# One hybrid layer with a mixture of experts: router on x, two-best choice by maximum and index instructions, token numbers scattered by GpSimd

## What is computed

```python
x = x + m                                             # m: the mixer's output projection
h = rmsnorm(x, norm_ffn_g)
gp = softmax(h @ w_router_group)                      # 4 groups
gidx, gval = argmax(gp), max(gp)
el = (h @ w_router_expert).reshape(-1, 4, 8)[gidx]    # the 8 experts of that group
tv, ti = top_k(softmax(el), 2); tv = tv / sum(tv)
for e in range(32):                                   # weighted by gval * tv where e was chosen
    out += combine[:, e] * ((silu(h @ w_gate[e]) * (h @ w_up[e])) @ w_down[e])
y = rmsnorm(x + out, norm_final_g)
```

## Time and profile before

| what | us |
|---|---|
| median of 3 runs (811.31 to 813.5) | 812.87 |
| the profiled execution, its own time | 813.58 |
| its span | 811.8 |
| TensorE products busy in the span | 776.9 |
| VectorE / ScalarE / GpSimd busy | 236.1 / 176.7 / 103.0 |
| DMA, mean over the span | 330 GB/s |

### The profile page before, as it was taken

The page is one execution under the profiler, slowest core; times in us unless marked ns, Lnnn a source line. Parts: engine busy times, 40 slices in busy tenths (PEclk is TensorE's granted clock), DMA queues, the critical chain, the costliest instruction groups (busy, mean ns, idle before and its releaser), DMA issues.

```text
span 811.8 us, 10142 instructions
## 1 busy us (share of the span) xinstructions
PE 776.9 (96%) x4170; PEld 447.5 (55%) x4170; DVE 236.1 (29%) x533; ACT 176.7 (22%) x321; POOL 103.0 (13%) x132
## 2 busy tenths in 40 slices
PE   8999999999999999999999999999998998999995
PEld 7888887888888888853333333333332332343332
DVE  4199869492551222531100111011101101101111
ACT  3104333657445000321111101100110010011001
POOL 5200064524200000001101000001000000000004
PEclk9999999999999999999999999999999999999998
DMA  9845587677849963599999999999999999999992
GB/s 328 239 141 192 162 244 217 174 212 195 260 139 385 401 249 146 195 346 429 422 427 397 424 428 424 428 427 424 429 423 430 428 425 426 422 428 422 419 417 82
DMA packets 75270, 268.03 MB, mean 330 GB/s; under 512 B 5710, under 2 KB 37562, under 8 KB 58447
## 3 DMA queue, kind: packets, MB, share of 16 engines
q1 hardware_dynamic: 73378, 264.26, 84.0%
q0 software_dynamic: 528, 1.90, 0.6%
q10 hardware_dynamic: 1317, 1.19, 0.5%
HBM read 259.26 MB, written 8.55 MB: 330 GB/s over the span
## 4 chain that ended last, share of the span: by engine, by line
PE 72%; DMA 14%; SPq 7%; DVE 2%; issue 2%; POOL 1%; ACT 1%; DVEq 0%; POOLq 0%
PE bank L1602 23%; PE bank L1979 19%; PE bank L2017 8%; SPq L537 7%; PE bank L1875 7%; DMA slot<-in_w_expert_gate_dram 5%; DMA slots<-in_w_expert_gate_dram 5%; PE bank L2026 4%; DMA early<-in_norm_final_g_dram 3%; PE bank L1822 2%; DMA slots<-in_w_in_dram 1%; PE bank L1712 1%; PE bank L1943 1%; PE bank L1634 1%; PE bank L2006 1%
## 5 line engine op out<-in xcount | busy, mean ns | idle before, releaser
L1602 PE MATMUL bank<-hT,slots 128*128 128x264 f32 x832 | 189.6, 388 | 0.0
L1979 PE MATMUL bank<-slots,hT 128*64 128x512 f32 x624 | 180.0, 601 | 5.8 <-DMA slots<-in_w_expert_gate_dram 4.1
L1602 PEld LDWEIGHTS bank<-hT,slots 128*128 128x128 f32 x832 | 156.8, 190 | 26.6 <-issue 0.6
L1460 DVE TENSOR_TENSOR early<-early,bank 128x512 f32<-128x512 f32 x16 | 11.0, 687 | 383.4 <-PE bank L1979 383.4
L1979 PEld LDWEIGHTS bank<-slots,hT 128*64 128x64 f32 x624 | 55.2, 138 | 101.4 <-issue 90.7
L2017 PE MATMUL bank<-slots,wrep 128*64 128x512 f32 x304 | 85.7, 595 | 4.2 <-ACT wrep L1028 4.0
L1979 PE MATMUL bank<-slot,hT 128*64 128x512 f32 x208 | 82.8, 594 | 1.6 <-DMA slot<-in_w_expert_gate_dram 1.6
L761 POOL COPY hT<-early 128x512 f32 x30 | 17.5, 612 | 375.4 <-PE bank L1979 290.2
L2026 PE MATMUL bank<-hT,diag 128*128 128x512 f32 x128 | 59.2, 605 | 0.2 <-ACT hT L1040 0.2
L2017 PEld LDWEIGHTS bank<-slots,wrep 128*64 128x64 f32 x304 | 26.9, 137 | 42.4 <-issue 35.3
L1200 DVE SCALAR_TENSOR_TENSOR slot<-slot,rows_buf 128x256 f32<-128x256 f32 x120 | 49.4, 487 | 0.0
(11 more groups left out here) (315 smaller groups left out, 827.0 us busy)
## 6 DMA issues: line engine op xcount, KB each, us to landing
slots<-in_w_expert_down_dram SPq DMA_DIRECT2D x17, 2048.0 KB, 32.3
slots<-in_w_expert_gate_dram SPq DMA_DIRECT2D x15, 2048.0 KB, 27.0
slots<-in_w_expert_up_dram SPq DMA_DIRECT2D x15, 2048.0 KB, 32.0
slots<-in_w_in_dram SPq DMA_DIRECT2D x13, 2048.0 KB, 9.9
slots<-in_w_expert_gate_dram SPq DMA_DIRECT2D x10, 1024.0 KB, 27.3
slot<-in_w_expert_gate_dram SPq DMA_DIRECT2D x5, 2048.0 KB, 31.5
slot<-in_w_expert_up_dram SPq DMA_DIRECT2D x5, 2048.0 KB, 27.5
slot<-in_w_expert_down_dram SPq DMA_DIRECT2D x5, 2048.0 KB, 37.3
```

The source lines that it names most:

```text
L1460: dve.tensor_tensor(act.rearrange("s (f c) -> s f c", f=FT), act.rearrange("s (f c) -> s f c", f=FT), bank[UP][:, :].rearrange("s (c f) -> ...
L1602: last = mm(out, w[:, a, t * P:(t + 1) * P], (hT if c else xgain)[:, a, :], start=(a == 0), stop=(a == KT - 1))
L1979: last = mm(out[sl, :], xe[:, a, sl], expert_view(p, kind, e, a // 4)[:, a % 4, :], start=(a == 0), stop=(a == KT - 1))
```

## The change

- The router's weights are multiplied by the norm's weight once, by GpSimd, and `route` multiplies `xT` by them. `hT` and `h_rows` are not made. The turned rows are rows of x times one over the root; the norm's weight, loaded once more in the order of the experts' rows (`gain8`), is applied where `xe` is made: by VectorE for pair 0, by GpSimd for the others, whose copies become products.
- The sum of squares is made by GpSimd.
- The two experts are found with `max` and `max_index`, three of each, instead of two `first_max`.
- `sel1` and `row_numbers` are gone. GpSimd scatters the token numbers to their places in a DRAM list `listed` with six indirect transfers (one for each token tile and pick), after the list was filled with zeros early in the kernel, and reads the list back into `list_at`, four numbers on each partition. A pick without a place goes to a spare place of its own.
- TensorE's order is: two turned groups, one seat, two turned groups, ranks, the last two turned groups, three seats. ScalarE makes the exponentials before the last two groups, and an exponential on one row ahead of "ms".
- SyncE issues load 18 before the token rows are stored and load 17 before load 19.

```diff
+LISTED = 5 * P
...
+        gain8 = vec[:, 68:76]
...
-        tok_id = sb("tok_id", [P, 3])
+        tok_id = sb("tok_id", [P, 3], I32)
+        list_pos = sb("list_pos", [P, 3, 2], U32)
...
+        top = flat(24).rearrange("p (a n) -> p a n", a=3)
+        top_desc = flat(6).rearrange("p (k a n) -> p k a n", k=2, a=3)
+        list_f = flat(6).rearrange("p (a k) -> p a k", a=3)
...
-        h_rows = nc.dram_tensor("h_rows", [P, KT, T], F32)
         tok_rows = nc.dram_tensor("tok_rows", [T, D], F32)
         tok_quad = nc.dram_tensor("tok_quad", [T, 4], F32)
+        listed = nc.dram_tensor("listed", [LISTED + 1 + 6 * P, 1], I32)
...
             for n, c in ((5, HO + 1), (6, WO), (7, WO + 1)):
-                if c == WO + 1:
-                    sp.wait_ge(xg_ready, KT)
-                    sp.dma_start(h_rows[:, :, :], hT[:, :, :]).then_inc(h_stored, 16)
                 sp.wait_ge(proj.ready, proj.written(stream[c][1]))
                 load_slot(n)
...
             load_half(16)
+            sp.wait_ge(seated, 1)
+            sp.wait_ge(x_kept, 1)
+            load_half(18)
             sp.wait_ge(*misc.read(("ht", 5)))
             sp.dma_start(tok_rows[0:SEQ, :].rearrange("(t p) d -> p t d", p=P), xrow[:, 0:2, :]).then_inc(rows_kept, 16)
             sp.dma_start(tok_rows[SEQ:T, :], xrow[0:NB, 2, :]).then_inc(rows_kept, 16)
-            sp.wait_ge(seated, 1)
-            sp.wait_ge(x_kept, 1)
-            load_half(18)
             sp.wait_ge(quad_ready, 1)
             sp.dma_start(tok_quad[0:SEQ, :].rearrange("(a p) k -> p a k", p=P), quad[:, 0:2, :]).then_inc(quad_kept, 16)
             sp.dma_start(tok_quad[SEQ:T, :], quad[0:NB, 2, :]).then_inc(quad_kept, 16)
+            sp.wait_ge(smalls_done, 1)
+            sp.wait_ge(quad_kept, 32)
+            load_half(17)
             sp.wait_ge(rows_kept, 32)
             sp.wait_ge(m_gathered, 2)
             load_half(19)
-            sp.wait_ge(smalls_done, 1)
-            sp.wait_ge(quad_kept, 32)
-            load_half(17)
             sp.dma_start(rows_buf[:, :], tok_quad[:, :].rearrange("t k -> (t k)").partition_broadcast(P)).then_inc(rows_ready, 16)
...
+            pool.iota(spare_id, pattern=[[P, 3], [3 * P, 2]], base=LISTED + 1, channel_multiplier=1,
                       allow_small_or_imprecise_dtypes=True).then_inc(c_misc, 1)
+            step(pool.iota(tok_id[:, :], pattern=[[P, 3]], base=0, channel_multiplier=1))
+            step(pool.memset(list_at[:, :], 0))
+            pool.dma_start(listed[1:LISTED + 1, :].rearrange("(p b) o -> p (b o)", p=P), list_at[:, :]).then_inc(list_clear, 16)
...
+            pool.wait_ge(wrout_in, 32)
+            pool.wait_ge(*misc.read("vec"))
+            pool.tensor_tensor(wrout[:, :, :], wrout[:, :, :], vec[:, 60:68].unsqueeze(2).broadcast_to([P, KT, NG + NE]),
+                               ALU.mult).then_inc(c_const, 1)
...
-            pool.wait_ge(proj.ready, proj.written(("wo", KT - 1)))
-            pool.wait_ge(xg_ready, KT)
-            pool.tensor_copy(x_samples, xT[:, :, SEQ:T]).then_inc(x_kept, 1)
-            pool.iota(row0, pattern=[[1, P]], base=1, channel_multiplier=0,
-                      allow_small_or_imprecise_dtypes=True).then_inc(slot_row_ready, 1)
-            pool.iota(row1, pattern=[[1, LATER]], base=P + 1, channel_multiplier=0,
-                      allow_small_or_imprecise_dtypes=True).then_inc(slot_row_ready, 1)
+            for d in range(1, KT):
+                pool.wait_ge(f_sq, d + 1)
+                if d == 1:
+                    pool.iota(row0, pattern=[[1, P]], base=1, channel_multiplier=0,
+                              allow_small_or_imprecise_dtypes=True).then_inc(slot_row_ready, 1)
+                else:
+                    pool.wait_ge(f_sum, d - 1)
+                pool.tensor_tensor(rstd, fsq[:, 0, :] if d == 1 else rstd, fsq[:, d, :], ALU.add).then_inc(f_sum, 1)
             pool.wait_ge(*misc.read("ms"))
             pool.tensor_tensor(rs[:, :], rs[:, :], power[:, :].broadcast_to([P, 3]), ALU.pow).then_inc(f_rstd, 1)
+            pool.wait_ge(*proj.read(("wo", KT - 1)))
+            pool.tensor_copy(x_samples, xT[:, :, SEQ:T]).then_inc(x_kept, 1)
...
+            pool.wait_ge(list_clear, 16)
+            pool.wait_ge(pos_ready, 1)
+            for t, (_, m) in enumerate(TOK_TILES):
+                for pick in range(2):
+                    pool.indirect_dma_start(listed[:, :], bass.IndirectOffsetOnAxis(ap=list_pos[0:m, t, pick:pick + 1], axis=0),
+                                            tok_id[0:m, t:t + 1], None).then_inc(list_out, 16)
+            pool.wait_ge(list_out, 96)
+            pool.dma_start(list_at[:, 1:], listed[P + 1:LISTED + 1, :].rearrange("(b p) o -> p (b o)", p=P),
+                           allow_slow_non_contiguous=True).then_inc(list_in, 16)
+            pool.wait_ge(list_in, 16)
             pool.wait_ge(rows_kept, 32)
-            pool.wait_ge(list_ready, 1)
             fetch_rows(1)
-            pool.wait_ge(h_stored, 16)
+            pool.wait_ge(vec_in, 16 * 8)
             pool.wait_ge(offs_ready, 1)
             for p in range(1, PAIRS):
                 at = [pool.value_load(offs[0:1, 2 * p + e:2 * p + e + 1], min_val=0, max_val=COLS - SLOTS) for e in range(2)]
                 pool.wait_ge(m_xall, 2 * BLOCK_OF[p] + 2)
                 pool.wait_ge(m_up, 2 * p)
                 for e in range(2):
-                    pool.tensor_copy(xe[:, :, e * SLOTS:(e + 1) * SLOTS], xall[:, :, bass.ds(at[e], SLOTS)]).then_inc(m_xe, 1)
+                    pool.tensor_tensor(xe[:, :, e * SLOTS:(e + 1) * SLOTS], xall[:, :, bass.ds(at[e], SLOTS)],
+                                       gain8[:, :].unsqueeze(2).broadcast_to([P, KT, SLOTS]), ALU.mult).then_inc(m_xe, 1)
...
+            se.activation(yrs[0:1, 2:3], eps[0:1, :], ACT.Exp)
...
+            for i in range(4):
+                turned_row(i)
             se.wait_ge(exp_in, 1)
             for t in range(3):
                 se.activation(gd[:, t, :], gd[:, t, :], ACT.Exp, scale=rs[:, t:t + 1]).then_inc(exp_out, 1)
             se.wait_ge(exp_in, 2)
             for t in range(3):
                 se.activation(er[:, t, :], ed[:, t, :], ACT.Exp, scale=rs[:, t:t + 1]).then_inc(exp_out, 1)
+            for i in (4, 5):
+                turned_row(i)
...
-            se.wait_ge(h_stored, 16)
-            se.wait_ge(offs_ready, 1)
-            second = se.value_load(offs[0:1, 1:2], min_val=0, max_val=SLOTS)
-            for j in range(2):
-                se.wait_ge(m_gathered, j + 1)
-                src = bank[GATHER[j]][:, :].rearrange("p (a c) -> p a c", a=4)
-                se.copy(xe[:, 4 * j:4 * j + 4, 0:SLOTS], src[:, :, 0:SLOTS]).then_inc(first_xe, 1)
-                se.copy(xe[:, 4 * j:4 * j + 4, SLOTS:], src[:, :, bass.ds(second, SLOTS)]).then_inc(first_xe, 1)
-                se.copy(xall[:, 4 * j:4 * j + 4, 0:P], src).then_inc(m_xall, 1)
+            gather_out(0)
...
-            def sum_squares(d):
-
-                dve.wait_ge(f_sq, d + 1)
-                wait_pos(dve, f_sum, d - 1)
-                dve.tensor_tensor(rstd, fsq[:, 0, :] if d == 1 else rstd, fsq[:, d, :], ALU.add).then_inc(f_sum, 1)
-
             for d in range(KT):
                 src = take(proj, ("wo", d))
                 if d == 0:
                     dve.wait_ge(x_copied, KT // 2 + 1)
                 dve.tensor_tensor(xT[:, d, :], src[:, 0:T], xT[:, d, :], ALU.add).then_inc(P_dve, 1)
-
-                dve.wait_ge(*proj.read(("wo", d)))
-                dve.tensor_scalar(hT[:, d, :], xT[:, d, :], vec[:, 60 + d:61 + d], None, ALU.mult).then_inc(xg_ready, 1)
-                if d >= 2:
-                    sum_squares(d - 1)
-            sum_squares(KT - 1)
             dve.wait_ge(logits_ready, 1)
+            dve.wait_ge(f_sum, KT - 3)
...
-            first_max(elm, e1, eq, p1, oh1, e_desc, NE)
-            step(dve.scalar_tensor_tensor(elm2, oh1, -3 * BIG, elm, ALU.mult, ALU.add))
-            first_max(elm2, e2, eq, p2, oh2, e_desc, NE)
+            for t in range(3):
+                last = dve.max(top[:, t, :], elm[:, t, :])
+            step(last)
+            for t in range(3):
+                last = dve.max_index(top_at[:, t, :], top[:, t, :], elm[:, t, :])
+            step(last)
+            step(dve.tensor_scalar(top_desc.rearrange("p k a n -> p a (k n)"), top_at[:, :, 0:2], -1.0, float(NE), ALU.mult, ALU.add))
+            e1, e2 = top[:, :, 0:1], top[:, :, 1:2]
+            step(dve.tensor_tensor(oh.rearrange("p k a n -> p (k a) n"), desc[:, :].unsqueeze(1).broadcast_to([P, 6, NE]),
+                                   top_desc.rearrange("p k a n -> p (k a) n").broadcast_to([P, 6, NE]), ALU.is_equal))
             dve.tensor_tensor(member, oh1, oh2, ALU.add).then_inc(member_ready, 1)
...
+            step(dve.scalar_tensor_tensor(list_f, quad[:, :, 0:2], 0.0, spare_id,
+                                          ALU.is_equal, ALU.mult))
```

(50 more changed lines are left out.)

97 lines of the change are left out of this document (43 added, 54 removed).

## The result

| | us, median | ratio to before | 95% |
|---|---|---|---|
| before, same chip | 812.09 (810.85 to 813.5) | | |
| changed | 820.64 (819.34 to 822.43) | 1.0117 | 1.0105 to 1.013 |

By the medians of this table the change costs 8.6 us (their quotient is 1.0105); the ratio in the table, 1.0117, makes it 9.5. No change was forecast. The time is inside the range, but in the part that I had kept for another cause. The profiled execution took 820.63 us around a span of 818.9, 7.1 longer than the span before.

A forecast was written before the change was run, and what follows sets the result against it. The prediction took the expert-weight stream as the bound, not TensorE. The mark 1.5 us earlier less 0.6 for small pieces gave 0.9 us gain: 813.58 - 0.9 = 812.7, so a median of 812.0; range 809.5 to 827.

The forecast's parts named there:

- New small pieces: Scattered and read-back 4-byte pieces on the DMA engines: at most 1.2 us, 0.3 in the hole, 0.6 taken.
- Its landing, which I put at 351.0: `tok_quad`'s store in SyncE's queue lands at 351.0 (350.8 to 352) and releases the half load that came at 353.70 before.
- The choice: VectorE's finding of the two experts: maximum and index instructions make it 1.6 us earlier, 0.2 at least.
- No clock fall near 362: TensorE, pair 0: without the one-column row-number products, the granted clock's fall in 362 to 364 goes too, 1.7 us.
- I take 0 for the root: Sum of squares moved to GpSimd: no change for the root and the scaled rows, 0.3 us either way.
- The value load on VectorE: Load ahead of the first expert input's two products: 0 to 2 us, 0.5 taken; past 0.7 it delays the first gate product.
- The rows: Block 1's rows, fetched through scatter and readback, arrive at 373.9; the stream allows until 376.9, 3.0 us of slack.
- Readback by turns: Rival, chance 0.30: each readback piece waits its queue turn, block 1's rows come late, 13.2 us slower, 826.
- Latency only: Rival, chance 0.08: slower scatters or round trips bring block 1's rows 5 to 8 us later, 815 to 818.
- Saves more: Rival, chance 0.17: stream holes near 342 and 351 shrink, making 4 us with the dropped store: 809.
- no effect: Rival, chance 0.1 within the fed case's 0.45: the load behind `tok_quad` starts as slowly, the mark stays, 813.
- the mark: Landing of `rows_buf`, taken to move the end equally if the stream is fed: 360.9 against 362.4, 1.5 us earlier.

The follow-up runs named there:

- e6: The changed kernel with the list's entries 64 bytes apart in DRAM instead of 4, still 528 writes of 4 bytes: 815.64 us, ratio 1.0053.
- e10: The changed kernel with list entries 64 bytes apart and SyncE's queue in the order of the kernel before: 811.55 us, ratio 1.0008.
- e1: The changed kernel without the six scatters and their wait, so its result is wrong: 815.34 us, ratio 1.0054.
- e3: The changed kernel with SyncE's queue in the order of the kernel before, scatters unchanged: 816.53 us, ratio 1.0064.
- e12: e10 with `quad` in spare memory, half 19 and two recycled loads ahead of `rows_buf`, and four products in TensorE's wait: 811.0 us, ratio 0.9999.
- e14: e12 with `tok_quad` turned on TensorE and stored in four pieces of 1,056 bytes instead of 264 of 16: 811.0 us, ratio 1.0009.
- e15: e14 with the list's entries 4 bytes apart again: 814.47 us, ratio 1.0042.

## Why the prediction was wrong, point by point

**The step that failed** is "New small pieces": "At most 1.2 us, 0.3 where they fall into the hole; I take 0.6." It took the time on the DMA engines for the price. That much was right: the pieces go quickly. The price is what 528 neighbouring writes of 4 bytes do to everything behind them: 5.2 us (1.0117 to 1.0053). A row of before could have warned of it: the earlier trace rows, 62 GB/s in 352 to 354, which I read as nothing but a wait.

**The second failed term** is "Its landing, which I put at 351.0". With the spacing mended (e6) half 17 still goes at 355.79 and not at 351.3. What the traces show of it: the seats end at 344.7 and not at 343.4, and the new order holds the token rows behind half 18 until 345.10, where the old order issues them at 342.82 (e10). Half 18 and the rows together also start slowly: 49 and 184 GB/s in 344 to 348, where e10, whose queue is nearly as empty before (70 in 342 to 344), moves 406 and 291. So the rows are out near 352.5 and not at 350; 264 pieces of 16 bytes follow them; and half 19, no longer ahead of half 17, can't use the time. The old order gives back 3.6 us (e6 to e10); the 0.08 points that are left are at the edge of what can be told from nothing.

**Right, and it didn't matter.** The choice: three maxima in 0.38 us, each index a load of 0.07 to 0.09 and a search of 0.18. From the first maximum to the end of `member` it is 1.92 us (335.69 to 337.61), where it was 3.46: 1.5 shorter, for 1.6.

```profile
335.69 0.38 DVE L1411 MAX8 ga<-ga 128x8 f32<-128x32 f32 x3
...
336.11 0.09 DVE L1414 MATCH_VALUE_LOAD places<-ga 128x8 f32 x1
336.19 0.18 DVE L1414 FIND_INDEX8 places<-ga 128x8 uint32<-128x32 f32 x1
...
337.35 0.26 DVE L1420 TENSOR_TENSOR ga<-ga 128x96 f32<-128x96 f32 x1
```

No clock fall near 362: the gate and up products of pair 0 are all done by 365.65 at the full clock. The first down products end at 374.9, for 373.0 forecast and 377.9 before. The products on GpSimd take 2.05 us for pair 1 and 35.1 for all fifteen, and for pair 1 they lie beside the combine, as forecast. The small work ends at 349.2, for 348. The early part moves no more than executions differ: the load before the router goes at 332.73, for 333.70 before, and at 331.79 to 332.96 in the other kernels with the change.

**Wrong, and small.** "I take 0 for the root": TensorE waits 0.45 us for GpSimd's sum, and the granted clock falls to 0.50 (1.2 of 2.4 GHz) behind it in this trace, though not in every one; the seats end 1.3 us late. The value load on VectorE: 1.48 us, for 0.5, and TensorE waits 0.98 for it. The rows: asked for at 367.45 and there at 378.2, forecast 373.9; TensorE waits 3.3 us, and the stream none, since it is 7 us late itself (418 GB/s in 386 to 396).

**The rivals.** "Readback by turns" (0.30) would have given 826 and is false: the readback lands 6.9 us after its issue, 7.2 in e1 without any scatter. "Latency only" (815 to 818) came nearest in size, but by another way: the scatters took 14 us to their landing for 12 reckoned, and the late rows cost the stream nothing. "Saves more" and "no effect" fall. None of my cases had `tok_quad`'s landing itself late, the one event that the mark hung on.

## What to carry to other kernels

Ask of a small store not only how long its pieces take on the DMA engines but where they land: numbers for a later readback can be given 64 bytes each, the least tried with 4-byte writes. When a load waits for a small store's landing, look for what else is written at that time by any queue, and take the buffer off that wait if a spare corner of memory can hold the small tensor. A saved store is worth nothing while the queue behind it waits for something else; here it left the queue empty (8 GB/s in 342 to 344). And a transfer that is ready goes ahead of one that still waits: the token rows stood 2.3 us behind half 18.

## What the runs showed of the hardware

- 528 writes of 4 bytes into some 2.4 KB and a spare stretch beside it slow the core's weight reads and hold back the landing of its other store: 45 GB/s for 6 us in e3, 2.3 us for an 8 KB packet (0.35 in 358 to 360 of the same trace), and a landing 4 us behind the last packet in the changed kernel. At 64 or 512 bytes apart: nothing that can be measured against no scatter at all, within some 0.2 points. Half the pieces, half the loss. With 264 writes of 16 bytes side by side 82 instead of 295 GB/s for 2 us (e12, e14), without an effect on the time that can be told from none.
- A gap of 0.45 us in TensorE's work near 334 is followed by a granted clock of 0.50 or 0.51 in 336 to 338 in eight of eleven traces; with four products in the gap it stays at 1.00 in four of four (e12 to e15).
- Why neighbouring writes are slow inside the memory no run shows, nor whether 16 or 32 bytes between 4-byte entries would do.
